# Recurrent stage of a two-layer trunk: the key convolution, two background pieces and the output gate change places in VectorE's and ScalarE's order

## What is computed

```python
def mlstm_mixer(h, w_in, conv_w, conv_b, i_bias, f_bias, head_norm_w, w_out):
    proj = jnp.einsum('bsd,de->bse', h, w_in).astype(jnp.float32)
    qk = jax.nn.silu(causal_depthwise_conv(proj[..., :2 * D], conv_w, conv_b))
    q, k, v = qk[..., :D], qk[..., D:] * (HEAD_DIM ** -0.5), proj[..., 2 * D:3 * D]
    o_pre, i_pre, f_pre = ...
    ...
    _, hc = lax.scan(mlstm_chunk_step, init, (chunks of q, k, v, ig, lf))
    hs = hs * lax.rsqrt(jnp.mean(hs * hs, axis=-1, keepdims=True) + RMS_EPS)
    gated = jax.nn.sigmoid(o_pre) * (hs * head_norm_w)
    return jnp.einsum('bsd,de->bse', gated, w_out)
```

## Time and profile before

| what | value |
|---|---|
| median of 3 runs | 1963.46 us |
| the profiled execution | 1964.01 us |
| its span | 1962.2 us |
| TensorE matmul busy | 1926.7 us, 98% |
| VectorE busy | 1344.6 us, 69% |
| ScalarE busy | 1067.7 us, 54% |
| mean granted clock of TensorE | 0.993 |
| recurrent stage, `turn(0)` to `turn(15)` | 755.1 to 1263.7 us |

### The profile page before, as it was taken

The page is one execution under the profiler, slowest core; times in us unless marked ns, Lnnn a source line. Parts: engine busy times, 40 slices in busy tenths (PEclk is TensorE's granted clock), DMA queues, the critical chain, the costliest instruction groups (busy, mean ns, idle before and its releaser), DMA issues. The chain is left out here.

```text
span 1962.2 us, 24457 instructions
## 1 busy us (share of the span) xinstructions
PE 1926.7 (98%) x8526; PEld 1542.1 (79%) x8526; DVE 1344.6 (69%) x2120; ACT 1067.7 (54%) x1825; POOL 89.9 (5%) x121
## 2 busy tenths in 40 slices
PE   9999999999999999999999999999999999999999
PEld 6678888888788788778878778877888888878876
DVE  5777565655678977775866766777665656577885
ACT  7655555553445446666655656745645455435433
POOL 0110000000000100110000110011000000000010
PEclk9999999999999999999999999999999999999999
DMA  5344343447633633342323343235334345753353
GB/s 210 109 163 155 118 177 118 177 179 298 214 92 92 200 106 106 110 151 87 99 85 97 111 147 100 83 119 185 115 146 149 146 149 215 294 187 97 103 188 128
DMA packets 79706, 285.00 MB, mean 145 GB/s; under 512 B 9408, under 2 KB 9536, under 8 KB 71136
## 3 DMA queue, kind: packets, MB, share of 16 engines
q1 hardware_dynamic: 64288, 239.96, 34.9%
q0 software_dynamic: 8320, 27.27, 4.3%
q10 hardware_dynamic: 6976, 16.21, 2.8%
HBM read 211.51 MB, written 71.89 MB: 144 GB/s over the span
## 5 line engine op out<-in xcount | busy, mean ns | idle before, releaser
L1821 DVE TENSOR_TENSOR w_lo<-raw,w_hi 128x1024 fp32r<-128x1024 f32 x132 | 162.6, 1232 | 152.6 <-ACT w_hi L1281 150.2
L1467 ACT CAST h_hi<-h_raw 128x512 fp32r<-128x512 f32 x188 | 116.5, 620 | 246.7 <-PE core L1022 149.1
L803 PE MATMUL bank<-x_hi,w_hi 128*128 128x512 f32 x560 | 228.5, 408 | 1.7 <-issue 1.2
L1281 ACT CAST w_hi<-raw 128x1024 fp32r<-128x1024 f32 x132 | 137.6, 1043 | 163.4 <-PE bank L805 52.3
L805 PE MATMUL bank<-x_hi,w_lo 128*128 128x512 f32 x560 | 223.4, 399 | 0.0
L804 PE MATMUL bank<-x_lo,w_hi 128*128 128x512 f32 x560 | 222.2, 397 | 0.0
L2076 DVE TENSOR_TENSOR h_lo<-h_raw,h_hi 128x512 fp32r<-128x512 f32 x188 | 129.8, 690 | 120.8 <-ACT h_hi L1467 120.5
L1020 PE MATMUL core<-h_hi,w_hi 128*128 128x512 f32 x464 | 183.3, 395 | 0.6 <-DVE y L2142 0.6
L1021 PE MATMUL core<-h_lo,w_hi 128*128 128x512 f32 x464 | 183.5, 396 | 0.0
L1022 PE MATMUL core<-h_hi,w_lo 128*128 128x512 f32 x464 | 183.3, 395 | 0.0
L1970 DVE TENSOR_TENSOR w_lo<-sums,w_hi 128x512 fp32r<-128x512 f32 x104 | 71.8, 690 | 100.4 <-ACT w_hi L1309 97.5
(11 more groups left out here) (334 smaller groups left out, 4411.2 us busy)
## 6 DMA issues: line engine op xcount, KB each, us to landing
raw<-weights SPq DMA_DIRECT2D x132, 512.0 KB, 3.3
h_pair_dram<-y SPq DMA_DIRECT2D x26, 1792.0 KB, 6.7
h_raw<-h_pair_dram SPq DMA_DIRECT2D x182, 256.0 KB, 2.8
w<-second_pairs SPq DMA_DIRECT2D x24, 768.0 KB, 4.4
raw_odd<-first_pairs SPq DMA_DIRECT2D x14, 1024.0 KB, 7.1
x_scratch<-y POOLq DMA_DIRECT2D x48, 256.0 KB, 2.5
raw<-first_pairs SPq DMA_DIRECT2D x12, 1024.0 KB, 7.1
xold<-x_scratch POOLq DMA_DIRECT2D x40, 256.0 KB, 3.5
```

What stands on the lines that cost most here:

```text
L803: nc.tensor.matmul(o, a, hi(t), start=(k == 0), stop=False)
L1281: nc.scalar.copy(w_hi[:, ROW[u] * T:(ROW[u] + 2) * T], raw[:, (n % RAW) * BLK:(n % RAW + 1) * BLK]).then_inc(hi_ready, 1)
L1467: nc.scalar.copy(h_slot(n)[0], h_raw[:, at % H_RAW, :]).then_inc(h_hi_ready, 1)
L1821: dve.tensor_tensor(w_lo[:, s], raw[:, (n % RAW) * BLK:(n % RAW + 1) * BLK], w_hi[:, s].bitcast(F32), ALU.subtract).then_inc(lo_ready, 1)
```

## The change

VectorE: `tick(j, 1)` and `conv(j, 1)` no longer stand ahead of `denominators(j-1)`. The convolution comes behind `normalize(j-1)` and the low half of the next block; `gate_head(j-1)` comes ahead of both pieces in every pass, where it stood ahead of the second one only at j = 4, 8 and 12. ScalarE: both pieces come behind `keys(j)`, and `output_gate(j)` ahead of it. Nothing is computed differently.

```diff
@@ ScalarE, lstm @@
                     split_hi(BLOCK["head", j, 2] + 1)
-                    tick(j, 1)
                     conv_input(j, 1)
                     value_copy(j)
                     head_norm(j - 1)
                     split_hi(BLOCK["head", j, 3] + 1)
+                    output_gate(j)
                     keys(j)
+                    tick(j, 1)
                     tick(j, 2)
-                    output_gate(j)
@@ VectorE, lstm @@
                     split_lo(BLOCK["head", j, 2] + 1)
-                    tick(j, 1)
-                    conv(j, 1)
                     denominators(j - 1)
                     normalize(j - 1)
                     split_lo(BLOCK["head", j, 3] + 1)
+                    conv(j, 1)
                     if j % HEADS:
                         rows_for(j)
-                    if j % FT == 0:
-                        gate_head(j - 1)
+                    gate_head(j - 1)
+                    tick(j, 1)
                     tick(j, 2)
-                    if j % FT:
-                        gate_head(j - 1)
```

## The result

The changed kernel takes 2006.6 us (median of 4 runs, 2001.52 to 2010.28) against 1963.64 for the kernel before (4 runs, 1962.75 to 1964.49): ratio 1.0218, 95% interval 1.0197 to 1.0240. The forecast was 2008. The profiled execution took 2010.28 us with a span of 2008.5, 46.3 more than the earlier trace rows. I compare it with the profiled execution of before.

The account below looks back on a forecast made before the run. TensorE was taken as the bound. 1964.0 less 25.4 of removed waits, plus 45.7 of added idle time and 24.0 of slow clock, gave 2008.3, stated as 2008 us, with a range of 1974 to 2024.

Parts of the forecast that it names:

- The four waits for `hnorm` go, -25.4: TensorE's waits in passes 2, 4, 10 and 12 vanish with the slow clock behind them, saving 25.4 us at most.
- The cover behind `hnorm` is 0.65 us, pieces beyond it are paid: VectorE's `w_lo` of (j+1, 1) ends 0.65 us before TensorE wants it; pieces of both ticks beyond that delay TensorE.
- j = 2, the all-reduce beside `w_lo` and the root: Contention with GpSimd's all-reduce makes `w_lo` 2.0 us late; the later root adds 0.5 in pass 3; sum 2.5.
- j = 4, 1.2 + 7.9: Output projection: the gate of head 3 comes 1.2 us late, block 1 7.9 late through pieces and old x's load; sum 9.1.
- j = 5 and 13 fit: No VectorE pieces there; despite ScalarE's root and table load, `w_lo` at j = 5 fits by 0.2 us.
- j = 7, 2.4: Two low parts on VectorE make the block behind the gate projection 2.4 us late.
- the 2.4 foretold at `turn(15)`: In pass 15 `turn(15)` follows after six matmuls, and `keys` and gate come 2.4 us late for it.
- j = 8, 0.5: Later `keys` delays `gate_weights` and the output projection's block 1 by 0.5 us, between 0 and 2.
- The clock, 24: Twelve added waits of 2 us or longer each cost 2.0 us of slow TensorE clock: 24 us, bounds 0 and 37.
- Rival 2: Waits come as laid out, but at 2 to 3 us each leave the clock at 2.4 GHz: 1984 us, chance 0.12.
- Table loads at nothing: ScalarE's extra 1.28 us table load in each of 15 passes is hidden; 19 us at most if not.
- What the text said would show it: `hnorm` waits only in the last head, waits for `w_lo`, longest in j = 4 and 12, pass 4 about 61 us.

Follow-up runs that it names:

- Kernel 9: Kernel before, with VectorE's two additions of j = 2, 10 behind the gate and both ticks of j = 4, 12 in the next pass's output projection: 1950.60 us.
- Kernel 8: Changed kernel with both ticks one pass later, behind the split of block (j+1, 1), and low parts of j = 7, 15 early: 1972.87 us.
- Kernel 1: Kernel before with only VectorE's conv(j, 1) moved behind normalize(j-1) and the low half of the next block: 1977.14 us, ratio 1.0074.
- Kernel 3: Changed kernel with the convolution back ahead of denominators(j-1) and output_gate back behind keys, so only the pieces stay moved: 1980.87 us, ratio 1.0093.
- kernel 5: Changed kernel with ScalarE's output_gate put back behind keys, ahead of both ticks: 2008.33 us, ratio 1.0230.
- Kernel 4: Changed kernel with VectorE's tick(j, 1), the two low parts, back ahead of denominators at j = 7 and 15: 2000.7 us, ratio 1.0196.
- kernel 7: Kernel before with idle copies on VectorE ending passes 5, 6, 13, 14: fourteen at j = 5, 13 and ten at j = 6, 14: 1985.49 us.
- kernel 6: Kernel before with idle copies on VectorE ending passes 5, 6, 13, 14: nine at j = 5, 13 and five at j = 6, 14: 1966.65 us.
- kernel 10: Kernel 9 with ScalarE's root, tick(j-1, 3), behind conv_input(j, 0) at j = 3 and 11: 1946.05 us, ratio 0.9916.

## Why the prediction was right, and where it was not

- *The four waits for `hnorm` go, -25.4.* Right: only the last head's 0.9 us is left. Kernel 9 removes these four by moving the pieces alone, and gets new ones of 1.6 us for `hnorm` in passes 3 and 11.
- *The cover behind `hnorm` is 0.65 us, pieces beyond it are paid.* Right as the changed kernel's mechanism. The waits ahead of the second projection were 1.98 (foretold 2.5), 0.70 (2.0), 1.94 (2.7) and 2.93 (3.4) for the pieces of j = 1, 2, 3 and 6, each 0.5 to 1.3 shorter. Kernel 8 takes the pieces away from there and wins most of it back. Kernels 1 and 3 show what the step left out: VectorE's order ahead of `w_lo` is one path and ScalarE's row is another, and that one is late where the first is in time. In pass 2 of the change a slower clock hides the second wait (see the clock below).
- *j = 2, the all-reduce beside `w_lo` and the root.* The wait of 0.70 stood under the bounds of 1.4. The price for contention was taken from a `w_lo` of 1.82 us that starts 1.5 us into an all-reduce; here the `w_lo` starts with the all-reduce and takes 1.23, and the all-reduce pays instead (last section). The part that I had put at 0.5 behind the root was the larger one, 1.67 us at the updates for `v_tok` and 0.51 more. The sum of the pass, 2.5, was measured as 2.9.
- *j = 4, 1.2 + 7.9.* 1.05 for `hid_lo` and 7.43 ahead of block 1; the load of old x held VectorE 1.02 us as laid out. The longest wait of the profile, as said.
- *j = 5 and 13 fit.* Both at 27.28. Kernel 1 shows what makes them fit: there the root stands between `keys` and the gate, with a table load on either side, and the pass behind takes 30.2 us. In kernel 5 the gate is behind `keys` again but ahead of the root, and that pass takes 27.6. So it is enough that the gate comes ahead of the root.
- *j = 7, 2.4.* This is the mis-sized term. I priced the two low parts by the weight block queued behind them on VectorE and did not ask who reads the low parts themselves. The gate projection does, and it waits for both tiles: 6.52 us, and the pass at a clock of 0.85. Kernel 4 shows it: with the low parts early 0.83 us is left. At j = 15, which has no gate projection behind it, the 2.4 foretold at `turn(15)` were 2.67.
- *j = 8, 0.5.* The wait ahead of the output projection's block 1 was 2.95 us, and 1.12 before: +1.8, inside the bounds of 0 to 2. It comes with the convolution (kernels 1, 3 and 5), from two sides. Counted from the pass's `turn`, the block's cast starts at +30.03 instead of +29.09, since `keys` waits for the convolution and has the gates' exponentials behind it. And TensorE asks 0.9 us sooner, at +29.5 instead of +30.4: `hnorm` and the low half behind it come earlier, and the wait of 0.52 us at 1011.16 of the kernel before is gone. So only about 1 us of it lengthens the pass, as in kernel 4, where pass 8 takes 55.4 at a clock of 1.00. The 56.9 of the change has the clock in it, 0.97.
- *The clock, 24.* The stage grew by 44.5 us. Its passes lie 74.7 us above the quiet lengths (49.7 for pass 8 here), and TensorE idled for 53.7 of them; before it was 30.2 and 17.0. That leaves 21.0 us for the clock, where 13.2 stood before; the sum had 24 and 12.4. Net, idle time grew by 36.7 us where the sum had 32.7, and the clock took 7.8 where it had 11.6: the total is met by two errors of 4 us with opposite signs. The average price of 2.0 for a wait of 3 us and more is confirmed by kernel 7, and kernel 6 shows next to none for 1.5 us and less. Of the twelve waits that I counted, those that the pieces of j = 2 and 10 cause fell apart into waits of 1.7 us and less, in passes at 1.00. Passes 4 and 7 cost 4.8 (64.9 less 49.7 and the waits of 1.94, 1.05 and 7.43) and 4.5, instead of 4.0 each. Rival 2, a clock that stays, did not come in the changed kernel.
- *Table loads at nothing.* Right by kernel 5.

What the sum had no place for: idle time and clock can stand in for each other. Pass 10 of the changed kernel is the twin of pass 2, and the two differ by 0.4 us in length:

```profile
1095.25:1126.69 31.44, 28.00 (x142) 22.89 (x141) 20.50 (x43) 24.89 (x43) 0.00 (x0) 1.00 0.25 84
```
```profile
1099.16 0.47 PE L803 MATMUL bank<-x_hi,w_hi 128*128 128x512 f32 x1 [1.99 <-issue]
...
1114.97 0.47 PE L803 MATMUL bank<-x_hi,w_hi 128*128 128x512 f32 x1 [1.16 <-issue]
```

Pass 2 has the first wait (1.98), a clock of 0.95 and no second wait; pass 10 has a clock of 1.00, waits 1.16 us ahead of the fourth block (and 0.30 at the updates) and is no shorter. In both, TensorE starts the fourth block 0.1 us after VectorE has its `w_lo` ready, 19.4 and 19.7 us behind the `turn` (802.25 and 1114.97). Kernel 5's pass 2 has waits of 1.97 and 1.15 at 1.00 and takes 31.04 us, the changed kernel's 31.08. So the other engines set the time of that block, and a slower TensorE only used up time in which it would have waited. The 21.0 us are therefore a split of the time and not what a steady clock would give back.

What the text said would show it did: pass 4 at 64.9 against "about 61", since that figure left out the slow clock that the sum had.

## What to carry to other kernels

When an operation is moved back in an in-order queue, price it twice: by what is now queued behind it, and by who reads its own result; the second was 4 us short here. Ask for the cover of each queue, not of the one that the diff touches most, since two engines hand on what one is late by. Where only two of sixteen passes carry the delay, move the pieces of those passes to where there is slack (here the output projection, 22 us long) and leave the rest of a tuned order alone.

## What the runs showed of the hardware

- The granted clock does not follow from the length of the one wait. Waits of 3.1 to 3.8 us cost 1.8 to 2.6 us each on top of themselves (kernel 7), waits of 0.8 and 1.5 us 0.2 (kernel 6). Between and below it went both ways: 1.98 us at 786.79 of the changed kernel stands in a pass at 0.95 and 1.99 us at 1099.16 in its twin at 1.00 (2.4 GHz throughout). 2.38 us in kernel 1 and 2.92 us in kernel 4 stand in passes at 1.00, and passes 3 and 11 of kernel 10, with the same waits of 1.1 and 0.5 us, were granted 0.94 and 1.00. I have no cause for that. The four executions of the changed kernel, 2001.52 to 2010.28 us, have clocks of 0.993 to 0.986, the faster the higher.
- In the rows of this case, of a `w_lo` on VectorE and an all-reduce over partitions on GpSimd, the one that starts later is the one that gets longer. Where the `w_lo` is there from the start (changed kernel, kernels 3, 9 and 10), it takes its 1.23 us and the all-reduce 4.3 instead of the 3.26 of the earlier trace rows:

```profile
815.26 1.23 DVE L1821 TENSOR_TENSOR w_lo<-raw,w_hi 128x1024 fp32r<-128x1024 f32 x1
```
```profile
815.27 4.32 POOL L1244 PARTITION_ALL_REDUCE tot<-acc  x1 [125.35 <-DVEq L1890]
```

Where it starts into a running all-reduce, the `w_lo` is longer: 1.82 us in the kernel before, beside an all-reduce of 3.23, and 2.05 in kernel 10, 2.35 us into one whose 4.31 is no longer than kernel 9's, which has no second `w_lo` in it:

```profile
809.64 2.05 DVE L1828 TENSOR_TENSOR w_lo<-raw,w_hi 128x1024 fp32r<-128x1024 f32 x1 [1.12 <-ACT w_hi L1281]
```

The quiet `w_lo` takes 1.22. The Trainium skill, "GPSIMD Engine Reference", section "1. Specifications", says that GpSimd's interfaces to SBUF are shared with VectorE and contend with instructions that have two SBUF inputs. This subtraction has two, and the rows agree; that section gives no price, and here it was 0.6 to 0.8 us for the `w_lo` or 1.1 us for the all-reduce.
